# A two-layer decoder trunk with top-2-of-8 experts on one core: 96 token slots per expert job in place of 128, five overflow rows in place of three, the overflow table moved from VectorE to GpSimd

## The reference, cut to what matters

```python
def _moe_swiglu(h, w_router, w_gate, w_up, w_down):      # h: 256 x 1024, hidden width 3584
    logits = (h @ w_router).astype(jnp.float32)
    top_val, top_idx = lax.top_k(logits, 2)
    top_w = jax.nn.softmax(top_val, axis=-1)
    combine = jnp.sum(jax.nn.one_hot(top_idx, 8) * top_w[..., None], axis=-2)
    out = jnp.zeros_like(h)
    for e in range(8):
        out = out + combine[..., e:e + 1] * _swiglu(h, w_gate[e], w_up[e], w_down[e])
    return out
```

## Time and profile before

| | |
|---|---|
| median of 3 runs | 1474.07 us (1472.14 to 1474.41) |
| span of the profiled execution | 1472.9 us (the page gives no other time of that execution) |
| PE, PEld busy | 1428.2 us (97%), 1219.7 us (83%) |
| DVE, ACT busy | 1135.9 us (77%), 1000.4 us (68%) |
| POOL busy | 43.5 us (3%) |
| mean granted TensorE clock | 0.989 |
| chain that ended last, by engine | PE 86%, DVE 6%, ACT 4%, issue 2%, DMA 1% |
| loads of expert weights | 336 of 1 MB |

### The profile page before, as it was taken

One profiled execution on the slowest core, in us unless ns is written; L12 is line 12 of the kernel. 1 busy time (PEld: TensorE's weight loads), 2 busy tenths in 40 slices (PEclk: granted clock), 3 DMA queues, 4 the chain that ended last, 5 costly groups with the idle time before them and its releaser, 6 DMA issues.

```text
span 1472.9 us, 19854 instructions
## 1 busy us (share of the span) xinstructions
PE 1428.2 (97%) x7508; PEld 1219.7 (83%) x7508; DVE 1135.9 (77%) x866; ACT 1000.4 (68%) x823; POOL 43.5 (3%) x70
## 2 busy tenths in 40 slices
PE   6999999999999799999999999999999999999997
PEld 6887899997898688888888888888888888888775
DVE  4466554445467698888888888888898888888997
ACT  4776534344677477777777777777777777777775
POOL 4100000000100100000000000000000000002000
PEclk9999999999999899999999999999999999999998
DMA  9834555554543499999999999999999999999993
GB/s 362 282 125 134 182 171 195 163 193 145 184 144 104 168 359 387 365 383 394 382 365 392 381 365 395 386 364 392 380 372 390 389 376 372 386 382 379 394 357 119
DMA packets 188128, 447.53 MB, mean 304 GB/s; under 512 B 7568, under 2 KB 9752, under 8 KB 188080
## 3 DMA queue, kind: packets, MB, share of 16 engines
q1 hardware_dynamic: 182928, 429.94, 80.1%
q0 software_dynamic: 3856, 12.67, 2.3%
q10 hardware_dynamic: 1296, 4.26, 0.7%
HBM read 436.35 MB, written 10.49 MB: 303 GB/s over the span
## 4 chain that ended last, share of the span: by engine, by line
PE 86%; DVE 6%; ACT 4%; issue 2%; DMA 1%; ACTq 0%; SPq 0%; DVEq 0%
PE ps L1383 81%; ACT whi L532 2%; DVE wlo L916 2%; PE ps L1747 2%; DMA raw<-in_moe_w_up_dram 1%; PE ps L1402 1%; DMA raw<-in_w_in_dram 1%; PE ps L1530 1%; DVE y L938 0%; ACT L542 0%; PE ps L1714 0%; DVE y L1101 0%; DVE qkc L984 0%; PE ps L1515 0%; PE ps L1534 0%
## 5 line engine op out<-in xcount | busy, mean ns | idle before, releaser
L916 DVE TENSOR_TENSOR wlo<-raw,whi 128x2048 fp32r<-128x2048 f32 x405 | 925.9, 2291 | 271.8 <-ACT whi L532 269.8
L532 ACT ACTIVATE whi<-raw 128x2048 fp32r<-128x2048 f32 x405 | 777.1, 1919 | 381.5 <-PE ps L1383 362.8
L1383 PE MATMUL ps<-whi,xT_hi 128*128 128x512 f32 x1056 | 417.5, 395 | 2.8 <-DVE wlo L916 2.4
L1383 PE MATMUL ps<-wlo,xT_hi 128*128 128x512 f32 x1056 | 411.7, 390 | 0.0
L1383 PE MATMUL ps<-whi,xT_lo 128*128 128x512 f32 x1056 | 411.0, 389 | 0.0
L1383 PEld LDWEIGHTS ps<-whi,xT_hi 128*128 128x128 f32 x1056 | 198.3, 188 | 44.3 <-issue 4.0
L1383 PEld LDWEIGHTS ps<-wlo,xT_hi 128*128 128x128 f32 x1056 | 198.2, 188 | 42.2
L1383 PEld LDWEIGHTS ps<-whi,xT_lo 128*128 128x128 f32 x1056 | 198.5, 188 | 38.8
L1383 PE MATMUL ps<-whi,hid_hi 128*128 128x512 f32 (+1 forms) x536 | 210.8, 393 | 1.3 <-DVE hid_lo L1233 1.3
L1383 PE MATMUL ps<-wlo,hid_hi 128*128 128x512 f32 (+1 forms) x536 | 208.7, 389 | 0.0
L1383 PE MATMUL ps<-whi,hid_lo 128*128 128x512 f32 (+1 forms) x536 | 208.6, 389 | 0.0
(11 more groups left out here) (243 smaller groups left out, 734.2 us busy)
## 6 DMA issues: line engine op xcount, KB each, us to landing
raw<-in_moe_w_gate_dram SPq DMA_DIRECT2D x112, 1024.0 KB, 7.1
raw<-in_moe_w_up_dram SPq DMA_DIRECT2D x112, 1024.0 KB, 7.3
raw<-in_moe_w_down_dram SPq DMA_DIRECT2D x112, 1024.0 KB, 7.1
raw<-in_w_in_dram SPq DMA_DIRECT2D x28, 1024.0 KB, 8.5
raw<-in_ffn_w_gate_dram SPq DMA_DIRECT2D x10, 1024.0 KB, 5.1
raw<-in_ffn_w_up_dram SPq DMA_DIRECT2D x10, 1024.0 KB, 5.1
raw<-in_ffn_w_down_dram SPq DMA_DIRECT2D x10, 1024.0 KB, 4.9
raw<-in_w_out_dram SPq DMA_DIRECT2D x8, 1024.0 KB, 4.9
```

What stands on the lines that cost most here:

```text
L532: act.activation(whi[:, i % NSPLIT, :], raw[:, i % NRAW, :], ACT.Copy).then_inc(hi_ready, 1)
L916: dve.tensor_tensor(wlo[:, i % NSPLIT, :], raw[:, i % NRAW, :], whi[:, i % NSPLIT, :].bitcast(F32), ALU.subtract).then_inc(lo_ready, 1)
L1383: ins = pe.matmul(acc, lhs, rhs, start=start and m == 0, stop=stop and m == 2, skip_group_check=True)
```

## The change

A job has SLOTS = 96 slots. All tiles and instructions of a job that had 128 slots on the partitions or columns have 96: the loaded operands xT_hi, xT_lo, hid_hi and hid_lo have 96 columns, products are written to 96 partitions, and hidden and gathered rows are transposed from 96 partitions (with a 96 x 96 identity). The weight columns that stream stay 512. An expert may have up to two overflow jobs, EXTRA = 5 rows in all, so the loop at the end has five iterations. `count_extras`, three operations on VectorE, stands between `one_hot(0)` and `slot_numbers()`; the comparison at L1202 is gone. The table is worked out on GpSimd behind the scatters of x and ahead of the picks, with a wait behind every operation.

```diff
+SLOTS = 96
-EXTRA = 3
+EXTRA = 5
+HID = 4 * SLOTS
-DUMP = E * P
+DUMP = E * SLOTS
...
-                        sp.dma_start(x_slots, x_by_slot[bass.ds((e + 1) * P, P), :]
+                        sp.dma_start(x_slots, x_by_slot[bass.ds((e + 1) * SLOTS, SLOTS), :]
...
@@ gpsimd
+            def table_op(ins):
+                steps[0] += 1
+                ins.then_inc(table_step, 1)
+                pool.wait_ge(table_step, steps[0])
+            def sum_of(to, v):
+                for n in (4, 2):
+                    table_op(pool.tensor_tensor(v[:, 0:n], v[:, 0:n], v[:, n:2 * n], ALU.add))
+                table_op(pool.tensor_tensor(to, v[:, 0:1], v[:, 1:2], ALU.add))
+            pool.wait_ge(extras_counted, 1)
+            steps[0] = 0
+            made, upto, below = ovf[:, 0], ovf[:, 1], extra[:, 0]
+            table_op(pool.tensor_tensor(below, upto, made, ALU.subtract))
+            for r in range(EXTRA):
+                is_of, of, names, back = (extra[:, i] for i in (1, 2, 3, 4))
+                table_op(pool.tensor_scalar(is_of, upto, float(r), None, ALU.is_gt))
+                table_op(pool.tensor_scalar(of, below, float(r), None, ALU.is_le))
+                table_op(pool.tensor_tensor(of, of, is_of, ALU.mult))
+                table_op(pool.tensor_tensor(names, of, iota_e[:], ALU.mult))
+                sum_of(table[:, r:r + 1], names)
+                table_op(pool.tensor_scalar(back, below, float(r + 1), float(SLOTS), ALU.subtract,
+                                            ALU.mult))
+                for t in range(TT):
+                    table_op(pool.tensor_tensor(extra_t[:, 0, t], job_pos[:, t, 0:E], back, ALU.add))
+                    table_op(pool.tensor_tensor(extra_t[:, 0, t], extra_t[:, 0, t], of, ALU.mult))
+                    sum_of(job_pos[:, t, E + r:E + r + 1], extra_t[:, 0, t])
+                    table_op(pool.tensor_tensor(extra_t[:, 1, t], job_w[:, t, 0:E], of, ALU.mult))
+                    sum_of(job_w[:, t, E + r:E + r + 1], extra_t[:, 1, t])
+            table_op(pool.tensor_scalar(table[:, EXTRA:EXTRA + 1], upto[:, E - 1:E], float(E), None,
+                                        ALU.add))
+            pool.tensor_copy(table_i[:], table[0:1, :]).then_inc(table_ready, 1)
...
@@ scalar
-                act.activation(silu[:, 0:512], ps[:, 2 * (f % 2), :], ACT.Silu).then_inc(e_sil, 1)
+                act.activation(silu[0:SLOTS, 0:512], ps[0:SLOTS, 2 * (f % 2), :], ACT.Silu
+                               ).then_inc(e_sil, 1)
...
-                act.activation(hid_hi[:, f % 2, 0:512], ps[:, 4 + f % 2, :], ACT.Copy
+                act.activation(hid_hi[:, f % 2, 0:HID], ps[:, 4 + f % 2, 0:HID], ACT.Copy
...
@@ vector
-            own(dve.tensor_scalar(ovf[:, 0], ps[:, 5, 16:24], float(P), None, ALU.is_gt))
...
+            def count_extras():
+                own(dve.tensor_scalar(ovf[:, 1], ps[:, 5, 16:24], float(SLOTS), None, ALU.is_gt))
+                own(dve.scalar_tensor_tensor(ovf[:, 0], ps[:, 5, 16:24], float(2 * SLOTS), ovf[:, 1],
+                                             ALU.is_gt, ALU.add))
+                dve.tensor_tensor_scan(ovf[:, 1], ones[:, 0:E], ovf[:, 0], 0.0, ALU.mult, ALU.add
+                                       ).then_inc(extras_counted, 1)
...
-                    if with_table:
-                        if i == 6:
-                            extra_table()
-                        if i in (10, 14, 18):
-                            extra_row((i - 10) // 4)
-                        if i == 20:
-                            table_done()
...
             one_hot(0)
+            count_extras()
             slot_numbers()
...
@@ tensor
-                        ins = passes(ps[:, bank, :], xT_hi[:, kk, 0:P], xT_lo[:, kk, 0:P],
+                        ins = passes(ps[0:SLOTS, bank, :], xT_hi[:, kk, 0:SLOTS], xT_lo[:, kk, 0:SLOTS],
...
-                    ins = pe.transpose(ps[:, 4 + f % 2, k * P:(k + 1) * P],
-                                       prod[:, k * P:(k + 1) * P], ident[:])
+                    ins = pe.transpose(ps[:, 4 + f % 2, k * SLOTS:(k + 1) * SLOTS],
+                                       prod[0:SLOTS, k * P:(k + 1) * P], ident[0:SLOTS, 0:SLOTS])
...
-                    hs = slice((2 * half + kk) * P, (2 * half + kk + 1) * P)
+                    hs = slice((2 * half + kk) * SLOTS, (2 * half + kk + 1) * SLOTS)
-                    ins = passes(ps[:, 6 + c, :], hid_hi[:, f % 2, hs], hid_lo[:, f % 2, hs],
+                    ins = passes(ps[0:SLOTS, 6 + c, :], hid_hi[:, f % 2, hs], hid_lo[:, f % 2, hs],
```

More of the change, by code:

```diff
@@ L158, in trunk @@
         job_w = sb("job_w", [P, TT, JOBS])
-        ovf = sb("ovf", [P, 8, E])
-        table = sb("table", [P, 4])
-        table_i = sb("table_i", [1, 4], I32)
+        ovf = sb("ovf", [P, 6, E])
+        extra = sb("extra", [P, 8, E])
+        extra_t = sb("extra_t", [P, 2, TT, E])
+        table = sb("table", [P, EXTRA + 1])
+        table_i = sb("table_i", [1, EXTRA + 1], I32)
         slot_in = sb("slot_in", [P, TT, 2], I32)
@@ L181, in trunk, with gathered_rows @@
         prod = scratch[:, 1024:2048]
-        slots = scratch[:, 2048:2304].rearrange("p (a t) -> p a t", a=2)
-        o_hi, o_lo = hid_hi[:, :, 512:], hid_lo[:, :, 512:]
+        slots = scratch[:, 2048:2048 + TT * SLOTS].rearrange("p (a t) -> p a t", a=TT)
+        o_hi, o_lo = hid_hi[0:SLOTS, :, 512:], hid_lo[0:SLOTS, :, 512:]
+        def gathered_rows(half):
+            return ps[:, 2 + half, 0:4 * SLOTS].rearrange("p (c t) -> p c t", t=SLOTS)
         rows = [y[0:HM, r // 2, 256 * (r % 2):256 * (r % 2) + 256] for r in range(4)]
@@ L393, in _ @@
             sp.wait_ge(table_ready, 1)
-            jobs = sp.value_load(table_i[0:1, 3:4], min_val=E, max_val=JOBS)
+            jobs = sp.value_load(table_i[0:1, EXTRA:EXTRA + 1], min_val=E, max_val=JOBS)
             with sp.Fori(E, JOBS) as j:
@@ L881, in _ @@
             act.wait_ge(table_ready, 1)
-            jobs = act.value_load(table_i[0:1, 3:4], min_val=E, max_val=JOBS)
+            jobs = act.value_load(table_i[0:1, EXTRA:EXTRA + 1], min_val=E, max_val=JOBS)
             with act.Fori(E, JOBS) as j:
@@ L1218, in one_hot @@
                         else job_pos[:, t, (0, E - 1)[o]:(1, E)[o]]
-                    dve.tensor_scalar(slots[:, t, :], iota[:], at, None, ALU.is_equal
+                    dve.tensor_scalar(slots[:, t, :], iota[:, 0:SLOTS], at, None, ALU.is_equal
                                       ).then_inc(slots_ready, 1)
@@ L1232, in hid_low @@
                 dve.wait_ge(e_hid_hi, loop.at("block", f + 1))
-                dve.tensor_tensor(hid_lo[:, f % 2, 0:512], ps[:, 4 + f % 2, :],
-                                  hid_hi[:, f % 2, 0:512].bitcast(F32), ALU.subtract
+                dve.tensor_tensor(hid_lo[:, f % 2, 0:HID], ps[:, 4 + f % 2, 0:HID],
+                                  hid_hi[:, f % 2, 0:HID].bitcast(F32), ALU.subtract
                                   ).then_inc(e_hid, 1)
@@ L1724, in scatter_matrix @@
                 for t in range(TT):
-                    ins = pe.transpose(ps[:, 6, t * P:(t + 1) * P], slots[:, t, :], ident[:])
+                    ins = pe.transpose(ps[0:SLOTS, 6, t * P:(t + 1) * P], slots[:, t, :], ident[:])
                 ins.then_inc(scatT_ps, 1)
@@ L1826, in _ @@
             pe.wait_ge(table_ready, 1)
-            jobs = pe.value_load(table_i[0:1, 3:4], min_val=E, max_val=JOBS)
+            jobs = pe.value_load(table_i[0:1, EXTRA:EXTRA + 1], min_val=E, max_val=JOBS)
             with pe.Fori(E, JOBS) as j:
```

70 lines of the change are left out of this document (28 added, 42 removed).

## The result

| | before | after |
|---|---|---|
| median of 20 runs each | 1474.24 us | 1477.13 us (1475.26 to 1478.45) |
| ratio after / before | | 1.0015 [1.0009, 1.0021] |
| profiled execution: its time, its span | span 1472.9 us | 1477.51 us, span 1475.7 us |
| a middle job, gather to gather | 118.47 us | 119.13 us |

The change costs 2.2 us by the ratio and 2.9 us by the medians. By the bound of the prediction (0.2%) that is hardly told from no change. The forecast of 1466.2 us is missed by 11 us. Its range up to 1478 holds the result, but by luck: the upper end was there for a part of the third rival, GpSimd holding VectorE up, and that isn't what happened.

The account below looks back on a forecast made before the run. The prediction took TensorE, busy nearly all the span, to bound the kernel. Its terms, -3.8 - 5.5 + 0.2 + 1.2 = -7.9 us off the median of 1474.07, gave 1466.2 us, range 1458 to 1478.

Parts of the forecast that it names:

- third rival: GpSimd's 133 table operations hold up VectorE's splits beyond 0.31 us each; at 0.4 us, 12 us: 1478; chance 0.06.
- (b): Expert matmuls: 96 loaded columns shorten the pitch by 1.36 ns, times 4032: -5.5 us, bounds 0 and -13.5.
- 36-column row: Profile row of fp32r matmuls streaming 256 columns past 36 loaded: 116.1 ns, against 120.0 with 128; taken to exclude a loss.
- (c): Transposes of hidden and gathered rows: loading 128 columns sets their pitch, so 0; bounds 0 and -3.7 us.
- (a): Last job: overflow-row table work leaves VectorE, so TensorE's waits go: -3.8 us, bounds -2.5 and -4.9.
- (e): Loop over overflow rows at the end: two more empty iterations on ScalarE, +1.2 us, bounds +0.8 and +1.4.
- (d): Start of the expert stage: VectorE's added operations delay the first expert matmul: +0.2 us, bounds 0 and +0.5.
- (f): Transposes of 96 partitions among matmuls of 128: no drain of TensorE, 0; other bound +26.5 us.
- second rival: TensorE drains at each change between 128 and 96 partitions around 63 transpose groups: +26.5 us, 1492.7 us; chance 0.16.
- (g): Table on GpSimd: 133 small operations, 37 us alone, hidden before the seventh job's store: 0, up to +1 us.
- The first: Rival: expert matmul pitch doesn't move, leaving -2.4 us: 1471.7 us, from 1470 to 1473.5; chance 0.30.
- The rest of 0.03: Chance left over beside the forecast and its named rivals, treated as spread: 0.03.

Follow-up runs that it names:

- run 1: Changed kernel with 128 slots again, table on GpSimd and five overflow rows kept: 1472.28 us, ratio 0.9982 to before.
- run 3: Changed kernel, 96 slots, but gate, up and down matmuls load 128 columns, hidden column groups still 384 bytes apart: 1471.69 us, ratio 0.9976 to before.
- run 5: As run 3, 128 columns loaded, but hidden columns of each k laid 512 bytes apart and cleared once by VectorE: 1469.58 us, ratio 0.9949 to before.
- run 8: Kernel before, gate and up matmuls of blocks 1 to 4 streaming 256 columns twice past 128, 96, 64, 36 loaded; block 5 512 past 36: 1487.3 us.
- run 4: Kernel before, gate and up matmuls of blocks 1 to 6 loading 120, 112, 104, 96, 64 and 32 columns in place of 128: 1483.0 us.
- Run 9: Changed kernel with hidden columns of each k laid 128 apart, 96 of them loaded: 1474.0 us beside 1473.91.
- Run 7: Kernel before, transposes of hidden rows taking 128, 120, 112, 96, 80, 64 and 32 partitions and streamed columns block by block: 1475.1 us.
- run 6: Kernel before, gate and up matmuls of blocks 1 to 6 loading 128 columns from start column 128, 96, 64, 32, 16 and 8: 1486.0 us.

## Why the prediction was wrong, step by step

**(b), the pitch, failed, in its sign, and it decided the case.** The forecast had -1.36 ns a matmul. The changed kernel shows +2.9 for gate and up and +4.1 for down, some +13.2 us where -5.5 stood. Runs 1, 3 and 5 show the loaded columns as the cause. Three sentences of the step fell. "Streaming 256 or 512 columns ... the same fixed part, so I let it carry over": run 8 shows 96 columns at -4 ns with 256 streamed, and run 4 at +3 with 512. The were read rightly and were evidence for their own shape only. "I take the line through the two rows": run 4 shows no line, but 233.4 ns at 120 columns and about 229 at 104. "A loss is excluded by the 36-column row": it was not, and the bound of 0 should have been open on that side. The sign that the prediction named for itself, a middle job longer than 118.5 us, is there with 119.13. And the step never looked at the new addresses: slices 384 bytes apart. Run 9 prices that at 1 ns on 1344 matmuls, 1.2 to 1.5 us; in run 3, with 128 columns, it cost 3.5.

**(c), transposes, failed too, to the good side.** 0 was taken, -7.7 us measured (224 x 0.0275 + 7 x 0.22), beyond the bound of -3.7. The two together, 13.2 + 5.5 - 7.7 = 11.0 us, are the miss. "The load of 128 columns sets both": the earlier trace rows and the transposes have 109 and 110 ns, but not one cause. What would have told them apart is the PEld group, in after:

```profile
L1409 PEld LDWEIGHTS ps<-wlo,xT_hi 128*96 128x96 f32 x114 | 18.4, 161 | 7.8
...
L1773 PEld LDWEIGHTS ps<-ident,scratch 96*128 96x128 f32 x28 | 3.1, 140 | 1.1
```

The load of a transpose is a row of 140 ns in before as well, that of the logits' matmuls 192: not the same kind of load. Run 7 settles it for the transposes, 0.86 ns a streamed column; what sets the 109 ns of the logits' matmuls wasn't tested.

**(a), the table out of the last job, was right**: -3.8 forecast, -3.85 found (3.84 lost before, nothing after). Where VectorE still stalls, the picks, it was 0.8 in place of 1.2 us.

**(e), the empty iterations, was right**: +1.2, that is 0.60 us each. **(d), the start**: +0.2 forecast, +0.1 found.

**(f), no drain at 96 partitions, was right**; the second rival is out. Four transposes take 0.33 us and the matmul behind them follows as ever. The price of a drain, 0.21 us from the earlier trace rows, was sound too: run 7 has up to 0.18 with 64 rows, and none with 80 or 96. The Trainium skill, TensorEngine Tiling (Array Packing), Available Configurations, lists row modes of 32, 64 and 128; by that 80 and 96 rows run in the 128 mode, and the trace agrees.

**(g), GpSimd, was right in the total and wrong in its own duration.** "37 us alone" became 118.9: from 510.58 to 629.49 us. Timeline of POOL, then of DVE, in that stretch:

```profile
600.28 0.20 POOL L544 TENSOR_TENSOR extra_t<-job_w,extra 128x8 f32<-128x8 f32 x1
600.57 2.44 POOL L524 TENSOR_TENSOR extra_t<-extra_t 128x4 f32<-128x4 f32 x2
603.08 0.20 POOL L525 TENSOR_TENSOR job_w<-extra_t 128x1 f32<-128x1 f32 x1
```

```profile
597.86 2.29 DVE L964 TENSOR_TENSOR wlo<-raw,whi 128x2048 fp32r<-128x2048 f32 x1 [0.34 <-ACT whi L579]
600.07 0.68 DVE L1285 TENSOR_TENSOR scratch<-scratch,ps 96x512 f32<-96x512 f32 x1
600.67 2.28 DVE L964 TENSOR_TENSOR wlo<-raw,whi 128x2048 fp32r<-128x2048 f32 x1
```

While DVE reads raw and whi, both in SBUF, for wlo, two GpSimd operations on 128x4 elements take 2.44 us together; beside the product, with one operand in PSUM, one of 128x8 takes 0.20. wlo has a mean of 2.30 us meanwhile and 2.29 in the next job. That agrees with the rule of SBUF — State Buffer, Who interferes with whom, in the Trainium skill, by which the two contend for a shared port. The page lets either engine wait; here it was GpSimd. Nobody needs the table before the seventh job is stored, so it costs nothing. The third rival is out, and run 1 confirms it in the time.

**The rivals.** The third (GpSimd, 1478) came nearest in the total, for a wrong reason: VectorE wasn't held up. The first (pitch unchanged, 1471.7) was 5.4 us off. All rivals had the pitch at 0 or down; that it could go up stood in no case, and that is what happened. The rest of 0.03 was the only chance that it had.

**The sum of the bounds** was wrong as well. All low bounds of (a) to (e) add to -4.9 - 13.5 - 3.7 + 0 + 0.8 = -21.3, all high ones to -2.5 + 0 + 0 + 0.5 + 1.4 = -0.6. "With every bound" the case reaches from 1452.8 to 1473.5 us, not from 1458 to 1470.

What stays open is why: what in TensorE makes a matmul with under 128 loaded columns, or with a load from an address off 256 bytes, start later while its load is shorter or as long (188 ns with every offset of run 6), and why the sign turns at 256 streamed columns. It must also explain why the same shape has another pitch in the gate and the up product (112 columns, 229.0 and 233.3 ns) and in the last job. The PSUM partitions that a matmul writes change together with its loaded columns, so no run parts these two. The Trainium skill, TensorE: Matmul & The Clock Gate, Weight-path perf modes, states that a faster way of loading is on when the number of weights is 128 and the type isn't FP32. A step at 128 would fit that; the load rows of run 4, 188, 181, 174, 168, 161 ns for 128 to 96 columns, show none, so no run here bears it out.

## What to carry to other kernels

A slot count below 128 bought nothing on the loaded side: where 512 columns are streamed, load 128 columns whose start is a multiple of 256 bytes, even if a quarter of them is padding, and take the saving on the streamed side alone (transposes of 96 columns, 1 us a job). That turned +0.15% into -0.5%. A pitch that is measured at one streamed length is no witness for another, and two equal durations are no proof of one cause: compare the load rows before one is taken for the bound of the other. Work that nobody waits for can go to GpSimd even if it gets three times slower there.

## What the hardware showed that I had not expected

- A loss right below 128 loaded columns at 512 streamed: from 226.9 to 233.4 ns at 120 columns, and 228.9 to 230.1 from 104 to 64.
- The same narrow load has two pitches in two places: 112 columns 229.0 and 233.3 ns, 36 columns 226.7 and 230.4.
- At 256 streamed the same 96 columns are faster, 116.0 for 120.0 ns.
- 128 columns loaded from a start that is no multiple of 256 bytes: 232.4 to 233.4 ns for 226.7; from 256 and 512 bytes no loss.
- Small GpSimd operations beside VectorE's wlo: 1.4 us on the mean and up to 2.7 in place of 0.2.
